# Block products for 18 of 22 FFN chunks, with VectorE's order around them and the last four chunks' down projection rearranged

## The reference

```python
def conv_ffn(h, P, i):
    g = dwconv(h @ P['ffn_w_gate'][i], P['ffn_conv_w'][i])
    u = h @ P['ffn_w_up'][i]
    return (jax.nn.gelu(g) * u) @ P['ffn_w_down'][i]
...
        x = x + g2 * conv_ffn(h, P, i)
```

## Time and profile before

| | |
|---|---|
| median of 3 runs | 1918.06 us (1913.84 to 1918.71) |
| profiled execution | 1917.92 us, span 1916.2 us |
| mean granted TensorE clock | 0.989 |
| busy share of the span | PE 97%, VectorE 62%, ScalarE 36%, POOL 36% |
| longest chain of work | TensorE 86% of the span |

### The profile page before, as it was taken

One profiled execution on the slowest core, in us unless ns is written; L12 is line 12 of the kernel. 1 busy time (PEld: TensorE's weight loads), 2 busy tenths in 40 slices (PEclk: granted clock), 3 DMA queues, 4 the chain that ended last, 5 costly groups with the idle time before them and its releaser, 6 DMA issues.

```text
span 1916.2 us, 34733 instructions
## 1 busy us (share of the span) xinstructions
PE 1857.5 (97%) x13240; PEld 1775.7 (93%) x13240; DVE 1182.6 (62%) x2247; ACT 681.0 (36%) x1108; POOL 694.6 (36%) x389
## 2 busy tenths in 40 slices
PE   5999999999999999999999999999999999999997
PEld 3998888888999999999999999977899999999997
DVE  5767788776623777675554354567567676755543
ACT  4443332223313333333333321157433333333332
POOL 1232222223232336355335433433223363453352
PEclk9999999999999999999999999999999999999998
DMA  8335454554533212213212432211322232132221
GB/s 296 108 104 164 143 170 144 167 166 154 174 121 88 77 61 84 74 58 99 76 53 73 145 92 86 89 36 33 103 66 67 59 94 75 58 88 77 60 66 72
DMA packets 263965, 192.76 MB, mean 101 GB/s; under 512 B 25514, under 2 KB 247078, under 8 KB 263350
## 3 DMA queue, kind: packets, MB, share of 16 engines
q1 hardware_dynamic: 258694, 182.78, 31.2%
q10 hardware_dynamic: 5168, 8.58, 1.3%
HBM read 181.29 MB, written 10.04 MB: 100 GB/s over the span
## 4 chain that ended last, share of the span: by engine, by line
PE 86%; issue 5%; DVE 4%; ACT 2%; POOL 1%; DMA 1%; SPq 0%; POOLq 0%; ACTq 0%; DVEq 0%
PE ps L712 46%; PE ps L715 23%; PE ps L1044 5%; PE ps L782 2%; POOL w_lo L629 1%; PE ps L1190 1%; PE ps L974 1%; PE ps L1170 1%; PE ps L1136 1%; DVE x L2192 1%; DVE act_lo L1827 1%; DVE w_mix L2178 1%; ACT sp L1619 1%; PE ps L1209 0%; PE ps L959 0%
## 5 line engine op out<-in xcount | busy, mean ns | idle before, releaser
L629 POOL TENSOR_TENSOR w_lo<-raw,w_hi 128x1024 fp32r<-128x1024 f32 x212 | 532.0, 2513 | 1031.5 <-ACT w_hi L1243 1025.3
L712 PE MATMUL ps<-act_hi,w_hi 128*128 128x322 f32 x2752 | 640.5, 314 | 4.8 <-DVE act_lo L1827 2.2
L712 PE MATMUL ps<-act_lo,w_hi 128*128 128x322 f32 x2752 | 634.4, 312 | 0.0
L715 PE MATMUL ps<-act_hi,w_lo 128*128 128x322 f32 x2752 | 633.1, 311 | 0.0
L712 PEld LDWEIGHTS ps<-act_hi,w_hi 128*128 128x128 f32 x2752 | 462.4, 190 | 18.2 <-issue 14.9
L712 PEld LDWEIGHTS ps<-act_lo,w_hi 128*128 128x128 f32 x2752 | 464.2, 189 | 3.4 <-issue 3.4
L715 PEld LDWEIGHTS ps<-act_hi,w_lo 128*128 128x128 f32 x2752 | 467.0, 190 | 0.0
L1243 ACT ACTIVATE w_hi<-raw 128x1024 fp32r<-128x1024 f32 x212 | 222.7, 1052 | 250.1 <-PE ps L715 191.8
L1044 PE MATMUL ps<-quad_hi,w_hi 128*128 128x322 f32 x336 | 106.7, 318 | 8.4 <-DVE x L2192 8.4
L1911 DVE SCALAR_TENSOR_TENSOR ft<-fg,par,ft 128x642 f32<-128x642 f32 x44 | 110.6, 2514 | 3.5 <-DVE ft L1910 2.5
L2244 DVE TENSOR_TENSOR fg<-ps,spread 128x642 f32<-128x642 f32 x44 | 36.3, 826 | 115.1 <-PE ps L715 103.9
(11 more groups left out here) (326 smaller groups left out, 2533.3 us busy)
## 6 DMA issues: line engine op xcount, KB each, us to landing
ada<-in_ada_w SPq DMA_DIRECT2D x40, 1024.0 KB, 6.0
raw<-in_ssd_w_in SPq DMA_DIRECT2D x44, 512.0 KB, 3.9
raw<-in_ffn_w_gate SPq DMA_DIRECT2D x44, 512.0 KB, 3.8
raw<-in_ffn_w_up SPq DMA_DIRECT2D x44, 512.0 KB, 3.8
raw<-in_na_w_qkv SPq DMA_DIRECT2D x24, 512.0 KB, 3.7
raw<-in_ffn_w_down SPq DMA_DIRECT2D x32, 320.0 KB, 3.1
first<-in_ada_w SPq DMA_DIRECT2D x16, 512.0 KB, 11.1
raw<-in_mix_w_out SPq DMA_DIRECT2D x16, 512.0 KB, 4.1
```

The costliest lines, as they stand in the source:

```text
L629: g.tensor_tensor(w_lo[:, s], raw[:, s % RAW], w_hi[:, s], ALU.subtract).then_inc(S["low_split"], 1)
L712: t.matmul(half_out(2 * tset, h), hi, chunk_of(src, k0 + k, cols), start=start and src is src_hi, stop=False)
L715: mm = t.matmul(half_out(2 * tset, h), lo, chunk_of(src_hi, k0 + k, cols), start=False, stop=stop)
```

## The change

The block products take three parts, 18 chunks; four chunks stay plain. VectorE's order around a stretch changes: the weight sums of its second pair are made ahead of it, and the up half of the late chunk (`up_part`) behind it. A11 no longer updates x by itself; its copy is added to A12 in PSUM. The plain chunks' down projection makes two output tiles together, four slots of 2 chunks (128 KB loads) in the order first half of tile 0 and 1, second half of tile 0 and 1; `split` and `low` touch only the used 256 of 1024 columns there. `deferred_start(3)` moves ahead of the loop over the last chunks. In layer 1 the two tiles of a turn are turned between the slots of the next turn, and VectorE copies them out ahead of that turn's updates. In the mixer `sum_rows` holds the context chunk too, the row matmul is one of 512 columns, and the context rows use it with the rounded `pick` as the other operand. Context lines of the diff are left out:

```diff
@@ -47,7 +47,7 @@
...
-SPARTS = 2
+SPARTS = 3
@@ -255,8 +255,8 @@
...
-        sum_rows = [at("sum_rows0", N0 + 2 * ROW, [P, 2 * P], F32R),
-                    nc.alloc_sbuf_tensor_at("sum_rows1", [P, 2 * P], F32R, offset=tri_at + 2 * P * 4)]
+        sum_rows = mix("sum_rows", [P, NC * P], F32R)
+        assert o[0] <= N0
@@ -544,8 +544,8 @@
...
-                        k0 = F_PLAIN + (s % 2) * FB // 2
-                        weights(b, i, s, rows(ffn_w_down[lay], k0, k0 + FB // 2, (2 * i + s // 2) * P), FB // 2)
+                        k0 = F_PLAIN + (s // 2) * FB // 2
+                        weights(b, i, s, rows(ffn_w_down[lay], k0, k0 + FB // 2, (2 * i + s % 2) * P), FB // 2)
@@ -623,10 +623,11 @@
...
-            def low(b, i, s):
+            def low(b, i, s, nk=C):
...
-                g.tensor_tensor(w_lo[:, s], raw[:, s % RAW], w_hi[:, s], ALU.subtract).then_inc(S["low_split"], 1)
+                n = nk * P
+                g.tensor_tensor(w_lo[:, s, 0:n], raw[:, s % RAW, 0:n], w_hi[:, s, 0:n], ALU.subtract).then_inc(S["low_split"], 1)
@@ -653,9 +654,15 @@
...
-                    with pool.Fori(i0 + 1, (part + 2) * SP // 2 if part + 1 < SPARTS else (end - b) // 4) as i:
+                    with pool.Fori(i0 + 1, (part + 2) * SP // 2 if part + 1 < SPARTS else FC // 2) as i:
...
+                with pool.Fori(FC // 2, FFN_SLOTS // 4) as i:
+                    for s in range(4):
+                        low(b, i, s, FB // 2)
+                if b + FFN_SLOTS < end:
+                    for s in range(4):
+                        low(b + FFN_SLOTS, 0, s)
@@ -879,8 +886,8 @@
...
-            for n in range(LC):
-                bank, off = 4 + 3 * (n // 2), P + n % 2 * P
+            for n in range(NC):
+                bank, off = (4 + 3 * (n // 2), P + n % 2 * P) if n < LC else (4, 3 * P)
@@ -890,9 +897,7 @@
...
-                for b in range(2):
-                    mm = t.matmul(ps[:, 5, 2 * b * P:2 * b * P + 2 * P], lhs, sum_rows[b][:], start=True, stop=True)
-                mm.then_inc(S["rows_ready"], 1)
+                t.matmul(ps[:, 5, :], lhs, sum_rows[:, 0:LC * P], start=True, stop=True).then_inc(S["rows_ready"], 1)
@@ -955,8 +960,8 @@
...
-                        lhs = col[:, LC * KINDS + K_DA, r, h:h + 1].broadcast_to([P, P])
-                        mm = t.matmul(ps[:, 5, (2 * h + r) * P:(2 * h + r + 1) * P], lhs, tri[:, r, :], start=True, stop=True)
+                        lhs = pick[:, r, h:h + 1].broadcast_to([P, P])
+                        mm = t.matmul(ps[:, 5, (2 * h + r) * P:(2 * h + r + 1) * P], lhs, sum_rows[:, LC * P:NC * P], start=True, stop=True)
@@ -1032,10 +1037,10 @@
...
-                                          (A12, 2, 2), (S4, 3, 2), (A22, 6, 3)):
+                                          (A12, 2, 1), (S4, 3, 1), (A22, 6, 2)):
...
-                    pe.wait_ge(S["pair_taken"], 7 * pair + taken + TAKEN0)
+                    pe.wait_ge(S["pair_taken"], 6 * pair + taken + TAKEN0)
@@ -1066,31 +1071,29 @@
...
-                def down_tile(i, m, between=None):
...
-                    k = m % 2
+                def down_tiles(i, between=None):
...
-                        slot_ready(b, i, 2 * m + q)
-                        if q == 0:
-                            tile_free(tb, 2, i, m)
-                        elif between is not None:
-                            between()
-                        half_slot(k, (2 * m + q) % RING, range(FB // 2), f_hi, f_lo, q == 0, q == 1, k0=q * (FB // 2),
-                                  before=("ffn_ready", first + q * (FB // 2) + 1) if k == 0 else None
-                                  ).then_inc(S["slot_used"], 1)
+                        for m in range(2):
+                            slot_ready(b, i, 2 * q + m)
+                            if q == 0:
+                                tile_free(tb, 2, i, m)
+                            elif between is not None:
+                                between(m)
+                            half_slot(m, 2 * q + m, range(FB // 2), f_hi, f_lo, q == 0, q == 1, k0=q * (FB // 2),
+                                      before=("ffn_ready", first + q * (FB // 2) + 1) if m == 0 else None
+                                      ).then_inc(S["slot_used"], 1)
...
-                        for m in range(2):
-                            down_tile(i, m)
+                        down_tiles(i)
...
-                    down_tile(0, 0)
-                    with pe.Fori(0, C // 2 - 1) as i:
-                        for m in (1, 2):
-                            down_tile(i, m, between=lambda: turn_out(i, m - 1))
-                    down_tile(C // 2 - 1, 1, between=lambda: turn_out(C // 2 - 1, 0))
-                    turn_out(C // 2 - 1, 1)
+                    down_tiles(0)
+                    with pe.Fori(1, C // 2) as i:
+                        down_tiles(i, between=lambda m: turn_out(i - 1, m))
+                    for m in range(2):
+                        turn_out(C // 2 - 1, m)
@@ -1235,12 +1238,12 @@
...
-            def split(b, i, s):
+            def split(b, i, s, nk=C):
...
-                a(w_hi[:, s], raw[:, s % RAW], ACT.Copy).then_inc(S["high_split"], 1)
+                a(w_hi[:, s, 0:nk * P], raw[:, s % RAW, 0:nk * P], ACT.Copy).then_inc(S["high_split"], 1)
@@ -1441,18 +1444,18 @@
...
-            def tiles_added(n, b, tb, last_slot, splits):
...
-                def turn(i, splits):
+            def tiles_added(n, b, tb, splits):
...
+                def turn(i, splits, nk=FB // 2):
...
-                        if splits and not (n == 3 and s in last_slot):
-                            split(b + 4, i, s)
-                        if s in last_slot:
-                            k = last_slot.index(s)
+                        if splits and s < 2:
+                            split(b + 4, i, s, nk)
+                        if s >= 2:
+                            k = s - 2
...
-                            if splits and n == 3:
-                                split(b + 4, i, s)
+                            if splits:
+                                split(b + 4, i, s, nk)
@@ -1563,7 +1566,7 @@
...
-                            act.wait_ge(S["pair_taken"], TAKEN0 + 7 * (pair - 1) + 2)
+                            act.wait_ge(S["pair_taken"], TAKEN0 + 6 * (pair - 1) + 4)
@@ -1979,11 +1982,11 @@
...
-                    for b in range(2):
-                        row = ps[0:2 * HEADS, 4 + 3 * b, P:3 * P]
-                        st.did(v.memset(sum_rows[b][:].bitcast(F32)[4 * HEADS:P, :], 0.0))
-                        st.then_wait(v.tensor_copy(sum_rows[b][0:2 * HEADS, :], row))
-                        st.did(tt(sum_rows[b][2 * HEADS:4 * HEADS, :], row, sum_rows[b][0:2 * HEADS, :], ALU.subtract))
+                    st.did(v.memset(sum_rows[:].bitcast(F32)[4 * HEADS:P, :], 0.0))
+                    for bank, c0, c1, off in ((4, 0, 2 * P, P), (7, 2 * P, 4 * P, P), (4, 4 * P, 5 * P, 3 * P)):
+                        row = ps[0:2 * HEADS, bank, off:off + c1 - c0]
+                        st.then_wait(v.tensor_copy(sum_rows[0:2 * HEADS, c0:c1], row))
+                        st.did(tt(sum_rows[2 * HEADS:4 * HEADS, c0:c1], row, sum_rows[0:2 * HEADS, c0:c1], ALU.subtract))
@@ -2180,7 +2183,7 @@
...
-                more = q < PAIRS - 1
+                more = 0 < q < PAIRS - 1
@@ -2196,15 +2199,14 @@
...
-                    dve.wait_ge(S["pair_taken"], TAKEN0 + 7 * pair + n)
...
+                    dve.wait_ge(S["pair_taken"], TAKEN0 + 6 * pair + n)
...
+                used_product(S2)
...
-                to_x(A11, 0, 0).then_inc(S["pair_taken"], 1)
-                used_product(S2)
...
-                taken(2)
+                taken(1)
@@ -2220,13 +2222,15 @@
...
+                summed = ps[:, banks[A12], 0:SW]
+                st.then_wait(tt(summed, summed, first_sbuf[:], ALU.add))
...
-                taken(4)
+                taken(3)
@@ -2236,8 +2240,7 @@
...
-                def product(i, k):
...
+                def gate_part(i, k):
@@ -2248,9 +2251,10 @@
...
-                    if k == 1 and isinstance(i, int) and i < F_PLAIN // 2 and i % SK == SK - 1:
-                        for j in range(4):
-                            weight_sum((lay * SPARTS + i // SK) * PAIRS, j)
...
+                def up_part(i, k):
...
+                    n = f + k + 1 + 2 * i
@@ -2285,23 +2293,35 @@
...
+                    part, ends = i // SK, i % SK == SK - 1
+                    p0 = (lay * SPARTS + part) * PAIRS
...
-                            quad_sums(i, k, product(i, k))
+                            gate_part(i, k)
+                            if ends and k == 1:
+                                for j in range(4):
+                                    weight_sum(p0, j)
+                            quad_sums(i, k, up_part(i, k))
...
-                    if i % SK == SK - 1:
-                        part, late = i // SK, i + 1
-                        ins = product(late, 0)
```

(60 more changed lines are left out.)

## The result

The changed kernel takes 1925.61 us (median of 12 runs, 1922.26 to 1926.9) where the kernel before takes 1918.03 in the same comparison: ratio 1.0041, 95% interval 1.0032 to 1.005. It is slower, by a little more than the 0.3% that counts as a difference here. That lies in the range, 1907 to 1931, but it is the slow case (0.29), not the likeliest (0.45). The profiled execution took 1926.1 us, span 1924.3.

What follows compares the result with a forecast made beforehand. TensorE, busy for 97% of the span, was taken as the bound. From 1917.92 us, block products -10.7, pair waits -5.7, layer 0's down stage +13, layer 1's +8 and mixer rows -3.6 sum to +1.0: 1919 us, range 1907 to 1931.

Steps and rivals of the forecast that it cites:

- the slow case: Whole kernel slower than the forecast's 1913 to 1925 us; both slow-side rivals together, chance 0.29.
- The bound and the wait in the pairs: Block products: TensorE is the bound; six third-pair waits of 1.4 us, 8.4 in place of 14.1, -5.7 us.
- The up half behind the stretch: Late chunk's up half, under 4 us of VectorE, covered by the next gate tile's 7.1 us on TensorE; costed at nothing.
- the moved preparation: deferred_start passes into the loop before, where VectorE waits for TensorE; the first update no longer waits for it.
- The addition to A12: Block products: one PSUM addition of 322 columns on VectorE's path between S2 and S4, 0.5 us.
- Layer 0's down stage, +13: Last four plain chunks: three TensorE waits of 2.8 us, clock loss, about 3 us at the end; bounds +9 and +16.
- 0.5 each: Layer 0's down stage: 0.5 us of clock loss for each of three waits, as VectorE's chain absorbs part.
- the sign of being wrong: Forecast is wrong if clock 0.50 fills much of the down stages or of the third pair's wait.
- Layer 1, +8: Layer 1's down stage: three waits, 4.2 us, 2.1 after the last matmul, 0.5 a turn for clock; bounds +6 and +11.
- Slower, the clock: Down-turn and third-pair waits halve the clock each time: 1935 us, with half of them 1927; chance 0.17.
- Slower, VectorE and POOL: In the pairs, weight sums keep meeting POOL's subtractions and the pair wait is 2.4 us: 1930 us; chance 0.12.
- Faster: Down turns not held by the split; pair waits, mixer rows and layer 1 at their lower bounds: 1908.5 us; chance 0.26.

Runs made afterwards that it cites:

- the run with A11 alone: Against the changed kernel: A11's own two updates of x back, A12's addition taken out, orders as changed; 1920.0 us, ratio 1.0014 to the kernel before.

## Why the prediction was right, and where not

**The bound and the wait in the pairs.** Right. Six waits of 1.4 us, 8.4 in all, are the forecast's figures, and the path behind it was forecast as 7.4 us "at best" and one stretched operation, 0.45, on top. From 720.22 to 727.66 and S4's own 0.5 it took 7.9. The one stretched beyond the best case was the fourth sum, as the run with A11 alone shows, not one that met POOL's leftovers of the pair before. The term was still too good by 1.7 us: beside the wait itself a stretch loses some 0.27 us (38.96 - 37.29 - 1.40). "So I take no halving for 1.4 us" held in all six. The Trainium skill ("TensorE: Matmul & The Clock Gate", HAM oscillation) describes another case, a loop whose bursts of matmuls are shorter than the waits between them and which starts each burst at the low clock. Here 18.65 us of matmuls stand before each of these waits, and none of the six fell.

**The up half behind the stretch, costed at nothing, and the moved preparation.** Right: no wait of TensorE stands behind a stretch, and the move back changed nothing that shows in one run.

**The addition to A12, "0.5 us as the one of S3".** Too low. On the path it costs 1.0, since it moves what follows into POOL's next subtraction.

**Layer 0's down stage, +13.** The step that failed. Its mechanism was right, the update of the second tile behind the first tile's low part and squares, and the waits were as large as said, 3.04, 2.65 and 2.64 us for "I take 2.8":

```profile
1050.89 0.88 PE L719 MATMUL ps<-f_hi,w_hi 128*128 128x322 f32 x2 [3.04 <-DVE x L2145]
...
1075.15 0.54 PE L719 MATMUL ps<-f_hi,w_hi 128*128 128x322 f32 x2 [2.64 <-DVE x L2145]
```

The estimates under it held too: a load of 128 KB landed in 2.2 us (2.4 estimated), a subtraction of 256 columns took 0.74 (0.7). Two of its terms were mis-sized. The clock: "0.5 each" was a compromise, and in this profile two of the three waits halved it, one of them for 5.9 us (the third row is the stretch behind the stage):

```profile
1051.29:1057.20 5.91, 5.91 (x24) 0.51 0.15 44
1064.09:1067.50 3.41, 3.41 (x15) 0.53 0.00 0
...
1092.37:1101.40 9.03, 9.03 (x36) 0.50 1.01 324
```

What the waits leave of the stage's loss is 13.7 - 8.3 - 0.4 = some 5 us instead of 1.5; the two stretches at half clock are about 4.5 of them (5.91 x 0.49 + 3.41 x 0.47, an estimate). That is 9.3 of the stage's 42.45 us at half clock, near the sign of being wrong that the forecast named, clock 0.50 in much of a down stage. And the end, "about 1 us" and "about 2": it was 4.68 us and 9.0 us at half clock behind it, 7.6 in all, because ScalarE had a load's wait queued ahead of the seventh tile. The forecast looked for the subtraction of the QKV slot as the late one, and that was 0.43. Upper bound +16, measured +21.3.

**Layer 1, +8.** Too dear: +4.4, below the bound of +6. The second copy delays the first update, but TensorE waits only 0.25 us for that tile; with the second tile's wait a turn loses 1.03, 1.11 and 1.12 us where 0.6, 1.8 and 1.8 were forecast. No wait there halves the clock: it is 1.00 up to 1907.81, and the 0.90 of the stage comes from the end, 0.68 where the kernel before had 0.58. No experiment changes layer 1 alone, so this is read from the profile. And from the last matmul of the stage to the end it is 16.5 us (from 1907.81) where it was 15.9 (from 1900.36), 0.6 longer and not 2.1.

**The rivals.** "Slower, the clock" came nearest, 1927 for half of it, but in layer 0's down stage alone and never in the pairs. "Slower, VectorE and POOL" lives on as the A12 step. "Faster" needed the down stages at their lower bounds; only layer 1 went below its own.

**What luck did.** The misses of the terms are +0.6, 0, +1.7, +8.3 and -3.6. Layer 1's, which was too dear, pays for part of layer 0's; without it the time would have been some 1929, still in the range. The range's low end, 1907, lies below what all the forecast's terms at their low ends give, 1908.4.

## What to carry to other kernels

When a stage gets narrower, its engines' queues lose the cover that hid their order: look in each queue for an instruction that frees a buffer standing behind one that only finishes work, and for a wait on a load ahead of work that someone else waits for. A cost that replaces another of the same size can be dearer if the old one lay in idle time and the new one on the path between two releases. Before a change is called a loss, put the queues in order and measure again: here the change went from +0.4% to -1.3%.

## What was not expected of the hardware

Equal waits do not have equal consequences for the clock. In the run with A11 alone the same three waits of the down stage, 2.95, 3.11 and 3.11 us, halved the clock not once:

```profile
1035.83:1074.85 39.02, 29.43 (x194) 1.00 0.22 63
```

Its stage took 39.02 us where the changed kernel's, with two halvings, took 42.45. Seven profiles have these three waits: the changed kernel's and those of the six runs that do not reorder the stage's updates and keep the narrow slots. In them 11 of 21 waits are followed by a stretch at half clock, 9 of the 14 of 2.95 to 3.15 us and 2 of the 7 of 2.61 to 2.65. The stage takes 39.0 us with no halving, 40.1 with one and 41.0 to 42.5 with two. So the clock's part of this term changes from profile to profile while the waits stay the same. What decides it the profiles do not show; it is left open.
